# A two-block transformer kernel: GpSimd casts the first weight unit, VectorE makes low parts in one stage, two orders are rewritten

## The chip, the cores and the metric

The program runs on 1 core of one Trainium2 chip. The metric is device time in microseconds (us) of the launch; lower is better. A profiled execution also gives a span, from its first to its last instruction.

## The reference, cut to what matters

Everything is float32, 512 tokens by 1024 features. Two blocks follow each other.

```python
h = rmsnorm(x, norm_mix)
q, k, v, r, lr_f, lr_b, u, g_a, g_b = split(h @ w_in)         # lr_f, lr_b: 16 columns each
log_a_f = log_sigmoid(lr_f @ w_decay_up_fwd + b_decay_fwd) / 16   # and the same backward
...                                                            # gated linear attention, pooling
x = x + merged @ w_out
gate, up = split(rmsnorm(x, norm_ffn) @ w_ffn_in)              # 2 x 2816 columns
x = x + (silu(gate) * up) @ w_ffn_out
x = rmsnorm(x, norm_final)
# second block
mod = silu(c) @ w_ada + b_ada                                  # shift, scale, gate
h = rmsnorm(x, norm_g) * (1 + scale) + shift
...                                                            # dilated attention, HGRN2
x = x + gate * (y @ w_out_2)
out = rmsnorm(x, final_g)
```

## The kernel before, in words

**Products in three parts.** A float32 product is made from matmuls in the fp32r format: each operand is split into a high part (a cast to fp32r) and a low part (the operand minus its high part), and a tile of the result is the sum of high x high, high x low and low x high. The activations' parts are `hhi` and `hlo`, eight slices of 128 features by 512 tokens. The weights come in 112 units of at most 128x2048 elements, 1 MB each. SP loads a unit into `raw[slot]`, two slots in turn. ScalarE casts it to `whi[slot]` (`split_hi`, L456), and GpSimd subtracts and writes `wlo[slot]` (`split_lo`, L460); for some units VectorE does that (`dve_low`, L1225). TensorE waits on the count `s_unit_lo` before it uses a unit and on `s_acc_free` before it writes one of four PSUM banks `acc`; four more banks, `M`, serve all else. Most units hold two tiles of 24 matmuls each (`pe_tile`, L482 to L484), 0.227 us apart.

All order is written by hand: each engine has one list of instructions and waits on semaphores. A wait blocks all that stands behind it on its engine.

**The start.** SP loads x in four tiles, then the narrow weights `wlr` (the 32 columns lr_f and lr_b), the first unit (q and k of head 0) into slot 0, twelve small rows of vectors and the second unit. GpSimd issues ten small loads. x is normalised, transposed on TensorE into eight banks (L1954), scaled by ScalarE into `hhi` (L716), and VectorE writes `hlo` (L1293), slice by slice. Between the transposes TensorE runs matmuls on the identity that no one reads (`keep_clock`, L1925). The order on TensorE is then: 8 `keep_clock` matmuls; the narrow projection (L1970), with the transposition of the vector rows (L1974) amid it; two matmuls for an attention bias (L1995, L1997); the high products of q (`first_hi`, L1982 and L1983: `whi` by `hhi` and by `hlo`); `lr_sum` (L2017), which sums the narrow projection; the high products of k; four matmuls that expand the decay (`decay`, L2011); and the low products of q and k (`first_lo`, L1989). Then `head_iteration(0)` follows: the two tiles of unit 2, with `decay(4)` and `decay(5)` behind the first and `decay(6)`, `decay(7)` behind the second; the values (unit 3, L505 to L507); and unit 4.

ScalarE, behind the slices of `hhi`, casts unit 1, copies rows, evicts the narrow projection (L725), evicts the bias (L727), casts unit 2, copies `lr3` (L731), and runs three functions on each decay matmul (L751 to L755). Behind the fourth of these it evicts q and k (L739) and only then casts unit 3 (`split_hi(act, 3, 0)`). The cast of unit 4 stands ahead of the last decay. VectorE turns each decay into a running sum (L1304 to L1312).

**The first FFN projection.** 22 units of two tiles, gate and up, 11 passes of two. On VectorE a unit's block is: `ada_tile` (four instructions, L1508 to L1515, that reduce a 1024x128 tile of `w_ada`), then fsg (L1525, L1527), faa (L1531) and alo (L1534), the two last for the second tile. TensorE runs one small matmul on each `ada_tile` result, `ada_tile` too (L2190), behind a unit's second tile; it waits for the sum. In the first pass the matmul for unit 0 stands behind the first tile of unit 1.

**The end.** The last projection, `out_part(h, a)`, works on halves h of the columns; for each half, a = 0 and a = 1 are the halves of the contraction, and each runs over four token tiles t, one PSUM bank each (L2444 to L2446). The same four banks serve both h, so tile t of h = 1 waits until VectorE has read the bank in `z_tile(0, t)` (L1801; L1803 adds the residual). `z_square` on ScalarE sums the squares of a tile (L1194). `y_first` on VectorE multiplies it by the gains (L1807); it waits for the squares, since both use the tile.

Of the kernel before, what the change touches and what calls it, by code (L numbers as in the profile page):

```python
# [7 lines left out]
P = 128  # L8
DM = 1024
L = 512  # L10
KT = DM // P
TT = L // P
# [3 lines left out]
LR = 2 * RANK  # L16
# [4 lines left out]
FT = D_FF // P  # L21
# [30 lines left out]
U_LR, U_HEAD, U_C, U_POOL, U_BR, U_OUT = 0, 1, 17, 23, 24, 28  # L52
# [60 lines left out]
def build(nc, inp, out):  # L113
# [18 lines left out]
    ident = at("ident", S0, [P, P])  # L132
# [114 lines left out]
    with ctx:  # L247
# [158 lines left out]
        def later(n):  # L406

            return not isinstance(n, int) or n > 0
# [15 lines left out]
        def x_bank(k):  # L424

            return acc[k] if k < 4 else M[k - 4]
# [46 lines left out]
        def raw_free(sp, u):  # L473
            if later(u - 1):
                sp.wait_ge(s_unit_lo, u - 1)
# [194 lines left out]
        def _(act):  # L670
# [49 lines left out]
            split_hi(act, 1, 0)  # L720
            act.wait_ge(s_col_mm, 2)
            A(vcol[:, KT:P], acc[3][:, KT:P], ACT.Copy).then_inc(s_cols, 1)
            b, full, _ = TL(U_LR, 0)
            act.wait_ge(s_acc_full, full)
            A(lrT[:, :], acc[b][:, :], ACT.Copy).then_inc(s_acc_free[b], 1)  # L725
            act.wait_ge(s_bias_mm, 2)
            A(brow[:, 0:L], M[3][0:A_HEADS, :], ACT.Copy).then_inc(s_bias_row, 1)  # L727
            A(brow[:, L:BW], M[2][0:A_HEADS, 0:BW - L], ACT.Copy).then_inc(s_bias_row, 1)
            split_hi(act, 2, 1)
# [458 lines left out]
            split_hi(act, U_OUT2 + 3, 1, lin=first_tile(U_OUT2) + TT)  # L1188
# [8 lines left out]
            for t in range(TT):  # L1197
                z_square(0, t)
# [14 lines left out]
        def _(dve):  # L1213
# [7 lines left out]
            def dve_low(u, slot):  # L1221

                dve.wait_ge(s_unit_lo, u)
                dve.wait_ge(s_unit_hi, u + 1)
                V.tensor_tensor(wlo[:, slot, :], raw[:, slot, :], whi[:, slot, :].bitcast(f32), ALU.subtract)\  # L1225
                    .then_inc(s_unit_lo, 1)
# [291 lines left out]
            with dve.Fori(0, FT // 2) as i:  # L1518
                for j in range(2):
                    ada_tile(i * 2 + j, j)  # L1520
                    bg, gfull, gfree = TL(U_FIN, 2 * j, 4, i)
                    bu, full, ufree = TL(U_FIN, 2 * j + 1, 4, i)
                    dve.wait_ge(s_norm_rs, 1)
                    dve.wait_ge(s_acc_full, gfull)
                    V.tensor_tensor(fsg[:, j, :], acc[bg][:, :], nrs[:, :], ALU.mult).then_inc(s_f_norm, 1)  # L1525
                    dve.wait_ge(s_f_sig, i * 2 + j + 1)
                    V.tensor_tensor(fsg[:, j, :], fsg[:, j, :], acc[bg][:, :], ALU.mult)\  # L1527
                        .then_inc(s_acc_free[bg], 1)
                    dve.wait_ge(s_acc_full, full)
                    dve.wait_ge(s_acc_free[bg], gfree + 1)  # L1530
                    V.tensor_tensor(faa[:, j, :], fsg[:, j, :], acc[bu][:, :], ALU.mult)\  # L1531
                        .then_inc(s_acc_free[bu], 1)
                    dve.wait_ge(s_f_hi, i * 2 + j + 1)
                    V.tensor_tensor(cols(alo, i * 2 + j), faa[:, j, :], cols(ahi, i * 2 + j).bitcast(f32),  # L1534
                                    ALU.subtract).then_inc(s_f_lo, 1)
            V.tensor_tensor(nrs[:, :], nrs[:, :], nrs[:, :], ALU.mult).then_inc(s_f_norm, 1)
# [277 lines left out]
            for t in range(TT):  # L1814
                z_tile(0, t)
                if t > 0:
                    y_first(t - 1)
            y_first(TT - 1)
# [10 lines left out]
        def _(pool):  # L1829
# [8 lines left out]
            for c in range(3):  # L1838
# [5 lines left out]
                          bass.AP(tensor=e.tensor, offset=0, ap=[[0, P], [1, NG * 2 * PAD]])).then_inc(s_edge_in, 16)  # L1844
            pool.wait_ge(s_wup_in, 6 * 16)
# [6 lines left out]
            split_lo(pool, 1, 0)  # L1852
# [19 lines left out]
            unit_pairs(U_BR, U_FOUT)  # L1872
            unit_pairs(U_FOUT, U_ATT, FT // 2 * P)
# [10 lines left out]
        def _(pe):  # L1884
# [75 lines left out]
            pe.wait_ge(s_lr_in, 32)  # L1960
            b, _, _ = TL(U_LR, 0)
            strips = P // LR
            pe.wait_ge(s_norm_lo, 1)
            keep_clock(acc[b], 8)
            for m in range(KT // strips):
                pe.wait_ge(s_norm_lo, (m + 1) * strips)
                for h in (hhi, hlo):
                    for c in range(strips):
                        k = m * strips + c
                        last = mm(acc[b][c * LR:(c + 1) * LR, :], wlr[:, k, :], h[:, k, :].bitcast(f32),  # L1970
                                  start=(m == 0 and h is hhi), stop=(m == 1 and h is hlo), skip_group_check=True)
                if m == 0:
                    pe.wait_ge(s_rows_in, 12 * 16)
                    nc.tensor.transpose(acc[3][:, 0:P], vrow[:, :], ident[:, :]).then_inc(s_col_mm, 1)  # L1974
                if m == 1:
                    last.then_inc(s_acc_full, 1)

            def first_hi(bank, j):

                for k in range(KT):  # L1980
# [11 lines left out]
            b_q, _, _ = TL(U_HEAD, 0)  # L1992
            b_k, _, _ = TL(U_HEAD, 1)
# [20 lines left out]
            pe.wait_ge(s_unit_hi, U_HEAD + 1)  # L2014
            first_hi(b_q, 0)
            pe.wait_ge(*moved(U_LR, 0))
            mm(M[0][:, :], lr_sum[:, :], lrT[:, :], start=True, stop=True).then_inc(s_lr3, 1)  # L2017
            first_hi(b_k, 1)
# [4 lines left out]
            pe.wait_ge(s_unit_lo, U_HEAD + 1)  # L2023
            first_lo(b_q, 0)
            first_lo(b_k, 1)
# [454 lines left out]
```

## Time and profile before

| what | value |
|---|---|
| median of 3 runs | 1352.64 us (1350.17, 1352.64, 1352.73) |
| the profiled execution, its own time | 1350.47 us |
| its span | 1348.7 us |
| TensorE busy | 1331.6 us, 99% of the span |
| TensorE weight loads | 1096.6 us, 81% |
| VectorE, ScalarE, GpSimd busy | 744.9, 573.8, 442.2 us |
| mean granted TensorE clock | 0.999 |

Times in a profile count from the start of the span. PE is TensorE's matmuls, PEld its weight loads, DVE is VectorE, ACT ScalarE, POOL GpSimd, and SP SyncE with its DMA queue. A number in square brackets behind an instruction is the idle time of its engine before it and what ended it. Matmul ends are modelled: a 512-column matmul shows as 0.39 us, while the next begins 0.227 us later.

### The profile page before, as it was taken

Reading aid. Unit: us, or ns where it says so; the run is one execution under the profiler, and the core shown is the slowest. Engines: PE = TensorE matmul, PEld = TensorE weight load, DVE = VectorE, ACT = ScalarE, POOL = GpSimd, SP = SyncE. Lnnn points to the kernel's source line nnn. Section 1 sums busy time; section 2 is a strip of 40 time slices with the busy share of each in tenths; the row PEclk is TensorE's granted clock in tenths of the full one; section 3 lists DMA queues with packets and bytes.
Section 4 is the critical chain, followed back from the end, with each engine's and each line's share of the span. In section 5 each row is a group of like instructions: output and inputs, shape, how many; then the busy total and the mean of one; then the engine's idle time right before and its main releaser. Section 6 shows DMA issues by size and latency. Waiting matters only on the chain.

```text
span 1348.7 us, 21206 instructions
## 1 busy us (share of the span) xinstructions
PE 1331.6 (99%) x8182; PEld 1096.6 (81%) x8182; DVE 744.9 (55%) x1243; ACT 573.8 (43%) x786; POOL 442.2 (33%) x118
## 2 busy tenths in 40 slices
PE   8999999999999999999999999999999999999997
PEld 6888989888888888888888877777888888888885
DVE  4643242664466888888844472335677777102445
ACT  5644353361243222222323255556555655433233
POOL 5421222234443444444444413322211111444441
PEclk9999999999999999999999999999999999999999
DMA  6231312214235555554433342232232222223221
GB/s 194 88 93 63 93 62 93 93 49 167 86 91 156 140 140 140 140 140 130 117 91 102 105 109 78 83 104 63 64 86 69 62 80 76 65 93 120 99 94 63
DMA packets 201671, 134.31 MB, mean 100 GB/s; under 512 B 5720, under 2 KB 195017, under 8 KB 201623
## 3 DMA queue, kind: packets, MB, share of 16 engines
q1 hardware_dynamic: 200390, 131.41, 33.4%
q10 hardware_dynamic: 848, 1.60, 0.4%
q8 instruction: 33, 0.54, 0.2%
q0 software_dynamic: 384, 0.64, 0.2%
q14 instruction: 16, 0.12, 0.0%
HBM read 131.51 MB, written 2.12 MB: 99 GB/s over the span
## 4 chain that ended last, share of the span: by engine, by line
PE 89%; issue 6%; DVE 2%; POOL 2%; ACT 0%; DMA 0%; POOLq 0%; DVEq 0%; ACTq 0%
PE acc L482 19%; PE acc L483 19%; PE acc L484 19%; PE acc L491 4%; PE acc L493 3%; PE acc L492 3%; POOL wlo L460 2%; PE acc L506 1%; PE acc L505 1%; PE acc L507 1%; PE acc L1905 1%; PE acc L1906 1%; PE acc L1907 1%; PE acc L2444 1%; PE acc L2446 1%
## 5 line engine op out<-in xcount | busy, mean ns | idle before, releaser
L460 POOL TENSOR_TENSOR wlo<-raw,whi 128x2048 fp32r<-128x2048 f32 (+1 forms) x97 | 427.2, 4404 | 864.9 <-ACT whi L456 864.8
L482 PE MATMUL acc<-hhi,whi 128*128 128x512 f32 x928 | 370.4, 399 | 1.9 <-issue 1.9
L484 PE MATMUL acc<-hhi,wlo 128*128 128x512 f32 x928 | 361.6, 390 | 0.0
L483 PE MATMUL acc<-hlo,whi 128*128 128x512 f32 x928 | 361.6, 390 | 0.0
L456 ACT ACTIVATE whi<-raw 128x2048 fp32r<-128x2048 f32 (+1 forms) x110 | 203.6, 1851 | 111.4 <-PE acc L484 92.0
L482 PEld LDWEIGHTS acc<-hhi,whi 128*128 128x128 f32 x928 | 174.3, 188 | 41.2 <-issue 6.5
L483 PEld LDWEIGHTS acc<-hlo,whi 128*128 128x128 f32 x928 | 174.4, 188 | 37.8 <-issue 3.1
L484 PEld LDWEIGHTS acc<-hhi,wlo 128*128 128x128 f32 x928 | 174.2, 188 | 36.7
L1511 DVE TENSOR_TENSOR ada<-ada 128x512 f32<-128x512 f32 x24 | 104.6, 4357 | 0.8
L491 PE MATMUL acc<-hhi,whi 128*128 128x512 f32 x224 | 92.7, 414 | 0.8 <-DVE wlo L1225 0.8
L493 PE MATMUL acc<-hhi,wlo 128*128 128x512 f32 x224 | 87.8, 392 | 0.0
L492 PE MATMUL acc<-hlo,whi 128*128 128x512 f32 x224 | 87.6, 391 | 0.0
L901 ACT ACTIVATE fsg<-fsg 128x512 f32<-128x512 f32 x22 | 13.9, 632 | 136.0 <-DVE fsg L1525 136.0
L482 PE MATMUL acc<-ahi,whi 128*128 128x512 f32 x176 | 68.7, 390 | 0.0
L484 PE MATMUL acc<-ahi,wlo 128*128 128x512 f32 x176 | 68.5, 389 | 0.0
L483 PE MATMUL acc<-alo,whi 128*128 128x512 f32 x176 | 68.5, 389 | 0.0
L491 PEld LDWEIGHTS acc<-hhi,whi 128*128 128x128 f32 x224 | 42.1, 188 | 12.8 <-issue 3.5
L493 PEld LDWEIGHTS acc<-hhi,wlo 128*128 128x128 f32 x224 | 42.0, 188 | 9.7
L492 PEld LDWEIGHTS acc<-hlo,whi 128*128 128x128 f32 x224 | 42.2, 188 | 7.5
L1548 DVE TENSOR_TENSOR ada<-acc,nrs 128x512 f32<-128x512 f32 x16 | 11.0, 690 | 51.6 <-PE acc L484 51.6
L484 PEld LDWEIGHTS acc<-ahi,wlo 128*128 128x128 f32 x176 | 33.0, 188 | 6.9
L482 PEld LDWEIGHTS acc<-ahi,whi 128*128 128x128 f32 x176 | 33.0, 188 | 6.8
(388 smaller groups left out, 2153.3 us busy)
## 6 DMA issues: line engine op xcount, KB each, us to landing
raw<-in_w_in_dram SPq DMA_DIRECT2D x56, 512.0 KB
raw<-in_w_in_dram SPq DMA_DIRECT2D x26, 1024.0 KB
raw<-in_w_ffn_in_dram SPq DMA_DIRECT2D x44, 512.0 KB
ada<-in_w_ada_dram SPq DMA_DIRECT2D x24, 512.0 KB, 3.8
raw<-in_w_ffn_out_dram SPq DMA_DIRECT2D x16, 704.0 KB
raw<-in_w_out_dram SPq DMA_DIRECT2D x8, 1024.0 KB
xnat<-in_x_dram SPq DMA_DIRECT2D x8, 512.0 KB, 6.3
raw<-in_w_branch_gla_dram SPq DMA_DIRECT2D x4, 1024.0 KB
```

The costliest lines, as they stand in the source:

```text
L456: nc.scalar.activation(whi[:, slot, 0:n], raw[:, slot, 0:n], ACT.Copy).then_inc(s_unit_hi, 1)
L460: nc.gpsimd.tensor_tensor(wlo[:, slot, 0:n], raw[:, slot, 0:n], whi[:, slot, 0:n].bitcast(f32), ALU.subtract).then_inc(s_unit_lo, 1)
L482: nc.tensor.matmul(acc[bank][:, :], h, xh[:, k, :], start=(k == 0), stop=False)
L483: nc.tensor.matmul(acc[bank][:, :], h, xl[:, k, :], start=False, stop=False)
L484: last = nc.tensor.matmul(acc[bank][:, :], lo, xh[:, k, :], start=False, stop=(k == nk - 1))
L491: nc.tensor.matmul(acc[bank][:, :], whi[:, slot, ws], hhi[:, k, :], start=(k == 0), stop=False)
L492: nc.tensor.matmul(acc[bank][:, :], whi[:, slot, ws], hlo[:, k, :], start=False, stop=False)
L493: last = nc.tensor.matmul(acc[bank][:, :], wlo[:, slot, ws], hhi[:, k, :], start=False, stop=(k == KT - 1))
L505: nc.tensor.matmul(o, xh[:, k, xs], h, start=(k == 0), stop=False)
L506: nc.tensor.matmul(o, xh[:, k, xs], lo, start=False, stop=False)
L901: A(fsg[:, j, :], fsg[:, j, :], ACT.Sigmoid).then_inc(s_f_sig, 1)
L1511: V.tensor_tensor(w[:, 0:4, :], w[:, 0:4, :], w[:, 4:8, :], ALU.add).then_inc(s_ada_step, 1)
```

## The change

- **Start.** GpSimd casts unit 1 to its high part itself, and makes its low part right behind, ahead of its work on `wup`. ScalarE's cast of unit 1 goes, and its cast of unit 2 comes first in its list, behind a wait for GpSimd's cast. TensorE makes the high products of q and k ahead of the narrow projection, in one loop over the rows k of `hhi` and `hlo`: four matmuls a row. The 8 `keep_clock` matmuls go. Then come the narrow projection, the vector rows, the bias, the low products of q, `lr_sum`, the low products of k, and the four decays. The x transposes use the banks in another order, so that the banks of q and k come free first.
- **Loads.** `raw_free` has no wait any more for unit 2; for all other units the wait is the same.
- **First FFN projection.** The low parts of its units from the third on, and of the first two of the second FFN projection, are made by VectorE, each at the end of a unit's block, so ahead of the next `ada_tile`. GpSimd skips them.
- **End.** VectorE runs all four `z_tile(0, t)` and then all four `y_first(t)`. ScalarE's cast of the last unit moves from ahead of the squares to behind the second.

```diff
@@ -423,7 +423,7 @@
-            return acc[k] if k < 4 else M[k - 4]
+            return acc[(1, 2, 0, 3)[k]] if k < 4 else M[k - 4]
@@ -471,7 +471,7 @@
         def raw_free(sp, u):
-            if later(u - 1):
+            if later(u - 2):
                 sp.wait_ge(s_unit_lo, u - 1)
@@ -717,16 +717,16 @@
-            split_hi(act, 1, 0)
-            act.wait_ge(s_col_mm, 2)
-            A(vcol[:, KT:P], acc[3][:, KT:P], ACT.Copy).then_inc(s_cols, 1)
+            act.wait_ge(s_unit_hi, 2)
+            split_hi(act, 2, 1)
             b, full, _ = TL(U_LR, 0)
...
             A(lrT[:, :], acc[b][:, :], ACT.Copy).then_inc(s_acc_free[b], 1)
+            act.wait_ge(s_col_mm, 2)
+            A(vcol[:, KT:P], acc[3][:, KT:P], ACT.Copy).then_inc(s_cols, 1)
             act.wait_ge(s_bias_mm, 2)
...
             A(brow[:, L:BW], M[2][0:A_HEADS, 0:BW - L], ACT.Copy).then_inc(s_bias_row, 1)
-            split_hi(act, 2, 1)
             act.wait_ge(s_lr3, 1)
@@ -1185,7 +1185,6 @@
             split_hi(act, U_OUT2 + 2, 0, lin=first_tile(U_OUT2))
-            split_hi(act, U_OUT2 + 3, 1, lin=first_tile(U_OUT2) + TT)
@@ -1195,6 +1194,8 @@
             for t in range(TT):
+                if t == 2:
+                    split_hi(act, U_OUT2 + 3, 1, lin=first_tile(U_OUT2) + TT)
                 z_square(0, t)
@@ -1218,11 +1219,11 @@
-            def dve_low(u, slot):
+            def dve_low(u, slot, n=16 * P):
...
                 dve.wait_ge(s_unit_hi, u + 1)
-                V.tensor_tensor(wlo[:, slot, :], raw[:, slot, :], whi[:, slot, :].bitcast(f32), ALU.subtract)\
+                V.tensor_tensor(wlo[:, slot, 0:n], raw[:, slot, 0:n], whi[:, slot, 0:n].bitcast(f32), ALU.subtract)\
                     .then_inc(s_unit_lo, 1)
@@ -1515,7 +1516,7 @@
             dve.wait_ge(s_silu_c, 1)
-            with dve.Fori(0, FT // 2) as i:
+            def gate_up(i, n=16 * P):
                 for j in range(2):
@@ -1533,6 +1534,11 @@
                                     ALU.subtract).then_inc(s_f_lo, 1)
+                    dve_low(i * 2 + (U_FIN + 2 + j), j, n)
+            with dve.Fori(0, FT // 2 - 1) as i:
+                gate_up(i)
+            gate_up(FT // 2 - 1, FT // 2 * P)
             V.tensor_tensor(nrs[:, :], nrs[:, :], nrs[:, :], ALU.mult).then_inc(s_f_norm, 1)
@@ -1813,9 +1819,8 @@
                 z_tile(0, t)
-                if t > 0:
-                    y_first(t - 1)
-            y_first(TT - 1)
+            for t in range(TT):
+                y_first(t)
             V.tensor_scalar(xss, aden[:, 0, :], 1.0 / DM, EPS, ALU.mult, ALU.add).then_inc(s_norm_rs, 1)
@@ -1842,6 +1847,9 @@
                           bass.AP(tensor=e.tensor, offset=0, ap=[[0, P], [1, NG * 2 * PAD]])).then_inc(s_edge_in, 16)
+            pool.wait_ge(s_unit_in[0], 32)
+            nc.gpsimd.tensor_copy(whi[:, 0, :], raw[:, 0, :]).then_inc(s_unit_hi, 1)
+            split_lo(pool, 1, 0)
             pool.wait_ge(s_wup_in, 6 * 16)
@@ -1849,7 +1857,6 @@
             pool.wait_ge(s_pool_prep, 5)
-            split_lo(pool, 1, 0)
             split_lo(pool, 2, 1)
@@ -1869,8 +1876,9 @@
-            unit_pairs(U_BR, U_FOUT)
-            unit_pairs(U_FOUT, U_ATT, FT // 2 * P)
+            unit_pairs(U_BR, U_FIN + 2)
+            pool.wait_ge(s_unit_lo, U_FOUT + 2)
+            unit_pairs(U_FOUT + 2, U_ATT, FT // 2 * P)
             split_lo(pool, U_ATT, 0)
@@ -1957,40 +1965,35 @@
+            b_q, _, _ = TL(U_HEAD, 0)
+            b_k, _, _ = TL(U_HEAD, 1)
+            pe.wait_ge(s_unit_hi, U_HEAD + 1)
+            for k in range(KT):
+                pe.wait_ge(s_norm_lo, max(k, 1) + 1)
+                for bank, j in ((b_q, 0), (b_k, 1)):
+                    h = whi[:, 0, k * 2 * P + j * P:k * 2 * P + (j + 1) * P]
+                    mm(acc[bank][:, :], h, hhi[:, k, :], start=(k == 0), stop=False)
+                    mm(acc[bank][:, :], h, hlo[:, k, :], start=False, stop=False)
+            def first_lo(bank, j):
+                for k in range(KT):
+                    lo = wlo[:, 0, k * 2 * P + j * P:k * 2 * P + (j + 1) * P]
+                    last = mm(acc[bank][:, :], lo, hhi[:, k, :], start=False, stop=(k == KT - 1))
+                last.then_inc(s_acc_full, 1)
...
             strips = P // LR
-            pe.wait_ge(s_norm_lo, 1)
-            keep_clock(acc[b], 8)
             for m in range(KT // strips):
-                pe.wait_ge(s_norm_lo, (m + 1) * strips)
                 for h in (hhi, hlo):
...
                                   start=(m == 0 and h is hhi), stop=(m == 1 and h is hlo), skip_group_check=True)
-                if m == 0:
-                    pe.wait_ge(s_rows_in, 12 * 16)
-                    nc.tensor.transpose(acc[3][:, 0:P], vrow[:, :], ident[:, :]).then_inc(s_col_mm, 1)
-                if m == 1:
-                    last.then_inc(s_acc_full, 1)
-            def first_hi(bank, j):
-                for k in range(KT):
-                    h = whi[:, 0, k * 2 * P + j * P:k * 2 * P + (j + 1) * P]
-                    mm(acc[bank][:, :], h, hhi[:, k, :], start=(k == 0), stop=False)
-                    mm(acc[bank][:, :], h, hlo[:, k, :], start=False, stop=False)
-            def first_lo(bank, j):
-                for k in range(KT):
-                    lo = wlo[:, 0, k * 2 * P + j * P:k * 2 * P + (j + 1) * P]
-                    last = mm(acc[bank][:, :], lo, hhi[:, k, :], start=False, stop=(k == KT - 1))
-                last.then_inc(s_acc_full, 1)
-            b_q, _, _ = TL(U_HEAD, 0)
-            b_k, _, _ = TL(U_HEAD, 1)
+            last.then_inc(s_acc_full, 1)
+            pe.wait_ge(s_rows_in, 12 * 16)
+            nc.tensor.transpose(acc[3][:, 0:P], vrow[:, :], ident[:, :]).then_inc(s_col_mm, 1)
             pe.wait_ge(s_bias_src, 32)
@@ -2011,18 +2014,15 @@
-            pe.wait_ge(s_unit_hi, U_HEAD + 1)
-            first_hi(b_q, 0)
+            pe.wait_ge(s_unit_lo, U_HEAD + 1)
+            first_lo(b_q, 0)
             pe.wait_ge(*moved(U_LR, 0))
             mm(M[0][:, :], lr_sum[:, :], lrT[:, :], start=True, stop=True).then_inc(s_lr3, 1)
-            first_hi(b_k, 1)
+            first_lo(b_k, 1)
             pe.wait_ge(s_pool_prep, 5)
...
                 decay(i)
-            pe.wait_ge(s_unit_lo, U_HEAD + 1)
-            first_lo(b_q, 0)
-            first_lo(b_k, 1)
```

## Rows read from the trace of the kernel before

**Rows 1.** The page, busy time by engine: us, share of the span, instructions
```profile
PE 1331.6 (99%) x8182; PEld 1096.6 (81%) x8182; DVE 744.9 (55%) x1243; ACT 573.8 (43%) x786; POOL 442.2 (33%) x118
```

**Rows 2.** Timeline of the start: start us, us, engine line op
```profile
13.01 0.60 PE L1954 MATMUL mid<-ident,xnat 128*128 128x128 f32 x4
...
14.65 2.02 PE L1925 MATMUL acc<-ident 128*128 128x128 f32 x16 [1.04 <-DVE hlo L1293]
...
15.30 0.54 POOL L1843 DMA_DIRECT2D edge<-in_edge_dram  x1
...
18.61 1.04 POOL L1846 CAST wup<-wup 128x1024 fp32r<-128x1024 f32 x1 [2.77 <-DMA wup<-in_w_decay_up_bwd_dram]
...
22.17 9.16 POOL L460 TENSOR_TENSOR wlo<-raw,whi 128x2048 fp32r<-128x2048 f32 x2
```

**Rows 3.** DMA view of 0 to 13 us: packets, MB, share of 16 engines
```profile
q1 hardware_dynamic: 4040, 3.42, 84.8%
```

**Rows 4.** Chain that ended last, 0 to 60 us: start us, us, what
```profile
19.17 1.92 PE acc L1970 x16
21.09 0.95 PE mid L1995 x2
22.26 0.43 PE acc L1982
...
26.15 0.86 PE mid L2017 x2
...
30.69 0.91 PE mid L2011 x4
31.59 3.63 PE acc L1989 x16
```

**Rows 5.** Timelines of 30 to 100 us (ScalarE, GpSimd) and 46 to 48 us (TensorE)
```profile
31.01 0.69 ACT L751 ACTIVATE lt<-mid,vcol 128x512 f32<-128x512 f32 x1 [3.36 <-PE mid L2011]
...
39.60 1.92 ACT L456 ACTIVATE whi<-raw 128x2048 fp32r<-128x2048 f32 x1
...
41.60 4.62 POOL L460 TENSOR_TENSOR wlo<-raw,whi 128x2048 fp32r<-128x2048 f32 x1 [9.60 <-ACT whi L456]
...
46.84 0.28 PE L505 MATMUL acc<-whi,hhi 128*128 128x256 f32 x1
```

**Rows 6.** Windows at both ends: busy us (count) of each engine, granted clock, DMA
```profile
3.40:3.80 0.40, 0.40 (x3) 0.40 (x3) 0.00 (x0) 0.00 (x0) 0.00 (x0) 1.00 0.97 369
...
7.40:7.80 0.40, 0.40 (x6) 0.40 (x5) 0.40 (x1) 0.37 (x2) 0.00 (x0) 1.00 1.07 440
...
1342.10:1344.80 2.70, 0.00 (x0) 0.00 (x0) 2.01 (x3) 1.94 (x5) 0.00 (x0) 1.00 0.52 194
1344.80:1348.70 3.90, 0.00 (x0) 0.00 (x0) 0.75 (x1) 0.73 (x2) 0.00 (x0) 0.51 0.54 202
```

**Rows 7.** First FFN projection, first pass: timeline; then the line view of L1225
```profile
425.06 1.03 DVE L1534 TENSOR_TENSOR alo<-faa,ahi 128x512 f32 x1 [0.82 <-ACT ahi L904]
...
428.45 0.29 DVE L1515 TENSOR_TENSOR ada<-ada 128x128 f32<-128x128 f32 x1
...
428.80 0.38 PE L2190 MATMUL mid<-one_col,ada 128*128 128x1 f32 x2
...
L1225 DVE TENSOR_TENSOR wlo<-raw,whi x12: 2280/2282/2286, 77.9 to 1135.8; 128x2048 fp32r<-128x2048 f32 x12
```

**Rows 8.** First FFN projection, a later pass: timeline of VectorE and TensorE
```profile
507.64 0.29 DVE L1515 TENSOR_TENSOR ada<-ada 128x128 f32<-128x128 f32 x1
...
508.29 0.28 PE L2190 MATMUL mid<-one_col,ada 128*128 128x1 f32 x2
```

**Rows 9.** Timeline of the end: VectorE, ScalarE and TensorE
```profile
1314.49 0.69 DVE L1803 TENSOR_TENSOR ynat<-ynat,xmn 128x512 f32<-128x512 f32 x1
...
1320.20 4.56 DVE L1807 TENSOR_TENSOR ynat<-ynat,gain_row 128x512 f32<-128x512 f32 x1 [5.02 <-ACT zsq L1194]
...
1317.64 1.92 ACT L456 ACTIVATE whi<-raw 128x2048 fp32r<-128x2048 f32 x1 [9.02 <-PE acc L2446]
...
1325.42 0.50 PE L2444 MATMUL acc<-whi,nhi 128*128 128x512 f32 x1 [2.43 <-DVE ynat L1801]
```

More of the change, by code:

```diff
@@ L1957, in _ @@
                         last.then_inc(s_x_tr, 1)
-            pe.wait_ge(s_lr_in, 32)
-            b, _, _ = TL(U_LR, 0)
-            strips = P // LR
-            pe.wait_ge(s_norm_lo, 1)
-            keep_clock(acc[b], 8)
-            for m in range(KT // strips):
-                pe.wait_ge(s_norm_lo, (m + 1) * strips)
[L1967 to L1971, printed above, removed]
-                if m == 0:
-                    pe.wait_ge(s_rows_in, 12 * 16)
-                    nc.tensor.transpose(acc[3][:, 0:P], vrow[:, :], ident[:, :]).then_inc(s_col_mm, 1)
-                if m == 1:
-                    last.then_inc(s_acc_full, 1)
-            def first_hi(bank, j):
-                for k in range(KT):
+            b_q, _, _ = TL(U_HEAD, 0)
[4 more added lines that the diff above has]
+                for bank, j in ((b_q, 0), (b_k, 1)):
                     h = whi[:, 0, k * 2 * P + j * P:k * 2 * P + (j + 1) * P]
@@ L1990, in first_lo @@
                 last.then_inc(s_acc_full, 1)
-            b_q, _, _ = TL(U_HEAD, 0)
-            b_k, _, _ = TL(U_HEAD, 1)
+            pe.wait_ge(s_lr_in, 32)
+            b, _, _ = TL(U_LR, 0)
+            strips = P // LR
+            for m in range(KT // strips):
+                for h in (hhi, hlo):
+                    for c in range(strips):
+                        k = m * strips + c
+                        last = mm(acc[b][c * LR:(c + 1) * LR, :], wlr[:, k, :], h[:, k, :].bitcast(f32),
+                                  start=(m == 0 and h is hhi), stop=(m == 1 and h is hlo), skip_group_check=True)
+            last.then_inc(s_acc_full, 1)
+            pe.wait_ge(s_rows_in, 12 * 16)
+            nc.tensor.transpose(acc[3][:, 0:P], vrow[:, :], ident[:, :]).then_inc(s_col_mm, 1)
             pe.wait_ge(s_bias_src, 32)
```

## Prediction

> **What bounds the kernel.** I read the page's busy times first: TensorE is busy for 99% of the span [rows 1]. So a step counts only if it makes TensorE start something later or earlier. The next views were the waits of TensorE, which hold one large entry, at the end [rows 9], then the timelines of the three stages that the change touches, and the chain of work for the start, which gives what each piece costs TensorE when nothing holds it up [rows 4]. After each stage I ask where TensorE stands against before; with 99% busy no later stage gives such a shift back, or takes it away.
>
> **Start, TensorE's own order.** The last transpositions of x end at 13.6 us [rows 2]. Before, TensorE went on at 14.65 with matmuls that no one reads, and then with the narrow projection. Now nothing may run until GpSimd has cast unit 1. GpSimd issues its last load until 15.84 [rows 2]. By 13 us SP's queue had moved 3.42 MB, which is x (2.1 MB), the narrow weights and nearly all of unit 1 (1.05 MB) [rows 3], so the cast waits for GpSimd's own queue. A cast of this size by GpSimd is not in the trace; one of half the size took 1.04 us [rows 2]. Bounds: 1.04 us if the size were free, 4.6 us if it cost what its subtraction of this size does (9.16 for two [rows 2]). I take 2.0, as it is the same operation. TensorE starts at 15.84 + 2.0 + 0.1 for the signal = 17.95. VectorE's slices of `hlo` do not hold it: the loop needs one per four matmuls, 0.9 us, and they are complete when the narrow projection could end before, at 19.17 [rows 4].
>
> From there, by the chain [rows 4]: 32 high products at 3.63 / 16 = 0.227 us, and 0.2 for the slow first: 7.5. The narrow projection, whose second half took 1.92: 3.84. The transposition of the vector rows: 0.2. The bias: 22.26 - 21.09 = 1.17. Low products of q 1.82, `lr_sum` 0.86, low products of k 1.82. The first decay starts at 17.95 + 17.2 = 35.2 instead of 30.69, **4.5 us later**, and the four end at 36.1 instead of 35.22. TensorE itself has lost only 0.9: it does the same work, and the fillers and gaps of before were what the order cost. GpSimd's moved work fits in: low part of unit 1 until 22.6, `wup` until 26, unit 2 until 30.7. SP's load of unit 3, which waits for the low part of unit 1, goes out some 4 us sooner, with nothing beside it.
>
> **Start, the chain behind the decay.** ScalarE's first function on a decay stood at 31.01; the fourth, the evictions of q and k, and the cast of unit 3 follow on it without a gap, and that cast began at 39.60. GpSimd's low part ran from 41.60 to 46.22, and TensorE began the values at 46.84 [rows 5]. The slack was 0.6 us. All of this hangs on the first decay, so it moves by 4.5: low part of unit 3 at 50.7, values at 50.8 instead of 46.84. **Cost 3.9 us**, of which 3.1 are a wait of TensorE for GpSimd that is new. Bounds: 0.9 if this chain were not in the way, and 6.5 if the cast took 4.6. The later units' chains move by the same, so nothing else comes late.
>
> **Start, the clock.** TensorE now idles from 13.6 to 17.95, 4.3 us. The trace shows what idling does once: after the last matmul the granted clock is 1.00 until 1344.8 and 0.51 from there, the lower of the two levels, 1.2 GHz for 2.4 [rows 6]. The stretch of 2.7 us ahead of that holds no matmul; the wait of 2.43 us at the end [rows 9] did not do it. So I expect the clock to fall here. How long it stays low: at the kernel's beginning the same filler matmuls run 3 in 0.4 us at 3.4 us and 6 in 0.4 us at 7.4 [rows 6] (the clock column reads 1.00 in both, but the pace is half), so between 1.0 and 4.6 us after the first matmul at 2.8. Half of that is lost: 0.5 to 2.3. I take **1.5 us**, all ahead of the first decay, so all of it counts.
>
> The Trainium skill (TensorE: Matmul & The Clock Gate, section on the HAM clock gate) says that the gate halves the clock once the engine has been idle, and gives it back after sustained work. By that rule the sum contains the loss; by the 2.43 us wait alone it would not. The trace agrees with the rule in the fall at its end.
>
> **Loads.** The wait that `raw_free` drops for unit 2 was for a count that a memset had given long before: nothing, from both sides.
>
> **First FFN projection.** In the steady passes VectorE's sum for `ada_tile` ended at 507.93 and TensorE asked for it at 508.29 [rows 8]. VectorE's low part costs 2.28 us [rows 7] and GpSimd's subtraction, behind which VectorE's instructions with both inputs in SBUF stood still (4.56 us for one that takes 0.69 [rows 9]), goes. So VectorE has more room than before, and TensorE, which waited for neither, gains nothing. The first pass is different. There the low part of the third unit stands ahead of the second `ada_tile`. Before, alo ended at 426.09 and the sum at 428.74, and TensorE used it at 428.80 [rows 7], when it came for it, give or take 0.1. Now: alo without the contention takes 0.69, so until 425.75; low part 2.28; the same 2.65 to the sum: 430.7. **Cost 1.9 us** of new waiting. Bounds: 0 if TensorE arrived 2 us later than I think, and 2.3 if alo is no faster. The next units' sums have more than 1 us to spare. Into the second projection a low part of VectorE ends about 5 us behind the first's last tile, and TensorE needs it after 7.5.
>
> **End.** TensorE waited 2.43 us for `z_tile(0, 2)` [rows 9], because VectorE was in `y_first(0)`, which waited 5.02 us for ScalarE's squares, which stood behind the cast at 1317.64, and then ran 4.56 us against GpSimd. Now VectorE is free from 1315.18 and reads the third and fourth banks as soon as they are full, the last by 1318.5; TensorE needs the third at 1322.8. The wait goes: 2.43, and 0.17 by which a matmul overlaps the next, **gain 2.6**. Next in line is the low part of the last unit, made as before. Bounds: 0 to 2.7. All that follows moves along, the tail behind the last matmul included.
>
> **Sum.** 3.9 + 1.9 - 2.6 = +3.2 us with the clock kept, and +4.7 with its fall. The profiled execution took 1350.47 (span 1348.7 and 1.8 around it): 1355.2 on its scale. The median of the runs, 1352.64, is 2.2 above it; the four executions stand at 1350.2, 1350.5, 1352.6 and 1352.7, and as I don't know which of these levels one of after takes, I add to their mean, 1351.5: **1356.2 us**.
>
> **Rivals.** 0.2%, 2.7 us, is about what a measurement of this kernel can tell from no change.
> - *The clock holds.* For it: the 2.43 us wait left it at 1.00. Against: 2.7 us of idleness ended in 0.51. +3.2: 1354.7. Chance 0.22.
> - *The chain behind the decay is not in the way*, because ScalarE or GpSimd reach unit 3 sooner than I read. Start 0.9, so 0.9 + 1.9 - 2.6 = +0.2: 1351.7. Against: 0.6 us of slack and no gap on ScalarE. Chance 0.08.
> - *The clock stays low for longer*, or falls again in the new 3.1 us wait for unit 3, at 2.3 for each: +7.8: 1359.3. For it: that wait is longer than 2.7. Chance 0.12.
> - *Faster: the steady FFN passes.* VectorE's sum came 0.36 us ahead of TensorE. If in the slower executions of before it comes late in each unit, the change takes that wait away. It decides from (2.7 + 4.7) / 20 = 0.37 us a unit. Against: no such wait in the profiled execution. At 0.4 a unit: -3.3, 1348.2. Chance 0.08.
> - My forecast, with its own range 1354 to 1358.5: 0.50.
>
> **How the numbers follow.** The range 1351.5 to 1360 holds the forecast, the held clock, the longer fall and the unhindered chain; it leaves out the faster case and extremes of the cast's price. Slower by over 0.2%: nearly all of the forecast, all of the longer fall, half of the held clock (+3.2 against 2.7): 0.69. Within: 0.22. Faster: 0.09.
>
> **What the profile after would show.** A gap on TensorE up to about 18 us behind a GpSimd CAST of 128x2048, and matmuls at 0.43 us behind it, if the clock fell. The first decay near 35 to 37. A wait of about 3 us for GpSimd's `wlo` ahead of the first values (L505's successor). A wait of 1.9 us at the second `ada_tile` matmul, none at the later ones. No wait at the end. The prediction fails if the cast is much quicker or slower than 2 us, if the values do not wait, or if the clock holds.

## The result, and the profile after

| | before | after |
|---|---|---|
| median of 14 runs, us | 1351.03 | 1354.24 |
| ratio of the times, 95% interval | | 1.0019 [1.0011, 1.0026] |
| profiled execution: time, span, us | 1350.47, 1348.7 | 1354.96, 1353.2 |
| mean granted clock in it | 0.999 | 0.994 |

The change makes the kernel slower, by 0.19%, which is 2.5 us; the interval lies clear of 1, and the size just under the bound of 0.2% of the forecast. The two medians lie 3.2 us apart; the ratio is not theirs, since before's runs stand in two groups and its median depends on how many fall in each. Two slow runs, one of before at 1658.25 us and one of the start alone (below) at 3440.33, are left out of the ratios. The forecast was 1356.2 with a range that holds 1354.24. The two profiled executions are 4.5 us apart, since that of before is of its lower group and that of after among its slower ones. After ran between 1351.02, at a mean clock of 0.998, and 1355.82, at 0.994, and the time goes with the clock: how often the clock fell makes most of that spread, as I infer, since only one run was profiled.

The page of after, busy time by engine:

```profile
PE 1332.9 (99%) x8166; PEld 1098.5 (81%) x8166; DVE 706.2 (52%) x1265; ACT 571.8 (42%) x785; POOL 345.4 (26%) x97
```

GpSimd's 97 us less and VectorE's 39 us less [rows 1] are no gain by themselves: TensorE is as busy as before. The waits of TensorE in after (total us, times, longest), without those of the kernel's first microseconds:

```profile
PE acc L1975 <- DVE hlo L1294: 4.2, 1, 4.2
...
PE acc L505 <- POOL wlo L460: 2.0, 1, 2.0
PE mid L2190 <- DVE ada L1516: 1.8, 1, 1.8
```

(The profile puts a wait down to the signal that it shows last.) The large wait at the end [rows 9] is gone, and three stand in its place. The first is put down to VectorE's `hlo`, but the timeline of after shows what the matmul waited for, the cast, and what followed:

```profile
15.84 1.90 POOL L1851 CAST whi<-raw 128x2048 fp32r<-128x2048 f32 x1
...
17.80 0.79 PE L1975 MATMUL acc<-hhi,whi 128*128 128x512 f32 x1 [4.18 <-DVE hlo L1294]
...
18.39 0.63 PE L1976 MATMUL acc<-hlo,whi 128*128 128x512 f32 x1
18.82 0.63 PE L1975 MATMUL acc<-hhi,whi 128*128 128x512 f32 x1
...
22.96 0.39 PE L1975 MATMUL acc<-hhi,whi 128*128 128x512 f32 x1
23.19 0.40 PE L1976 MATMUL acc<-hlo,whi 128*128 128x512 f32 x1
...
31.40 1.91 ACT L456 ACTIVATE whi<-raw 128x2048 fp32r<-128x2048 f32 x1 [13.72 <-PE acc L1992]
...
37.28 1.09 PE L2014 MATMUL mid<-lr,wup 128*128 128x512 f32 x4
...
46.36 1.92 ACT L456 ACTIVATE whi<-raw 128x2048 fp32r<-128x2048 f32 x1
...
48.35 4.57 POOL L460 TENSOR_TENSOR wlo<-raw,whi 128x2048 fp32r<-128x2048 f32 x1 [9.63 <-ACT whi L456]
...
52.98 0.39 PE L505 MATMUL acc<-whi,hhi 128*128 128x256 f32 x1 [1.98 <-POOL wlo L460]
```

The matmuls stand 0.43 us apart at 18.4 and 0.23 at 23.0: after 4.2 us of idleness the clock is at its lower level. The chain of the forecast is there step by step: first decay at 37.28 (before 30.69 [rows 4]), the cast of unit 3 at 46.36, its low part, and the values 0.06 us behind its end, at 52.98 instead of 46.84 [rows 5]. One thing I had not read in the diff: ScalarE's cast of unit 2 also waits for the count of finished tiles (`s_acc_full`), so until the narrow projection is done, and starts at 31.40. My forecast had its low part ready at 30.7. It came in time, by 0.15 us: its low part ended at 38.05 and TensorE took the unit up at 38.2.

Windows of after (busy us and count of PE, PEld, DVE, ACT, POOL; granted clock; DMA share; GB/s):

```profile
16.20:22.60 6.40, 4.80 (x11) 3.80 (x12) 2.90 (x5) 1.48 (x3) 6.32 (x3) 0.50 0.63 207
51.00:53.00 2.00, 0.02 (x1) 0.02 (x1) 1.97 (x3) 1.94 (x4) 1.93 (x1) 1.00 0.05 12
53.60:56.80 3.20, 3.20 (x17) 3.20 (x17) 3.04 (x4) 3.17 (x4) 0.94 (x1) 0.50 0.79 225
57.00:60.00 3.00, 3.00 (x27) 3.00 (x27) 2.86 (x4) 0.65 (x2) 3.00 (x1) 1.00 0.41 96
439.40:442.50 3.10, 3.10 (x9) 2.45 (x8) 1.96 (x3) 1.55 (x3) 0.00 (x0) 0.50 0.77 222
443.00:446.00 3.00, 3.00 (x15) 2.48 (x14) 2.40 (x2) 0.57 (x1) 0.00 (x0) 1.00 0.83 238
```

TensorE is busy throughout the third and the fifth row, but gets through 17 and 9 matmuls where the rows behind them have 27 and 15. Each stands half a microsecond to a microsecond behind a wait of 2.0 or 1.8 us. So the clock fell three times, not once; the second and the third fall lasted about 3.5 us, at a cost of some 1.6 us each. The unit in which the third fell took 12.90 us, and 11.31 in the kernels below in which the clock holds there.

The timeline of after in the first FFN projection: the first pass, then a turn of the loop.

```profile
432.78 0.69 DVE L1535 TENSOR_TENSOR alo<-faa,ahi 128x512 f32 x1 [0.83 <-ACT ahi L904]
433.39 2.28 DVE L1226 TENSOR_TENSOR wlo<-raw,whi 128x2048 fp32r<-128x2048 f32 x1
...
438.03 0.29 DVE L1516 TENSOR_TENSOR ada<-ada 128x128 f32<-128x128 f32 x1
...
438.38 0.38 PE L2190 MATMUL mid<-one_col,ada 128*128 128x1 f32 x2 [1.83 <-DVE ada L1516]
...
484.66 0.28 PE L2190 MATMUL mid<-one_col,ada 128*128 128x1 f32 x2
484.80 0.48 PE L482 MATMUL acc<-hhi,whi 128*128 128x512 f32 x1
...
495.79 0.28 PE L2190 MATMUL mid<-one_col,ada 128*128 128x1 f32 x2
```

The same turn before:

```profile
519.42 0.31 PE L2190 MATMUL mid<-one_col,ada 128*128 128x1 f32 x2
...
519.93 0.49 PE L482 MATMUL acc<-hhi,whi 128*128 128x512 f32 x1 [0.21 <-issue]
...
530.94 0.28 PE L2190 MATMUL mid<-one_col,ada 128*128 128x1 f32 x2
```

In the first pass the low part costs a wait of 1.83 us. In the passes behind it lies what I missed. After, a unit takes TensorE 11.13 us each time (484.66 to 495.79), and the matmul behind the `ada_tile` starts 0.14 later. Before, units took 11.13 and 11.52 in turn (508.29 [rows 8], 519.42, 530.94), with 0.51 us at the turn, a mean of 11.33. Over the 19 units that is 0.2 x 19 = 3.8 us. Among TensorE's waits of before it shows only in part, and with no releaser:

```profile
PE acc L482 <- issue: 1.9, 9, 0.3
```

The accounts of the two profiled executions, in us:

| term | predicted | profile of after |
|---|---|---|
| start, with the clock kept | +3.9 | +3.9 |
| fall of the clock at the start | +1.5 | +2.2 |
| second fall, behind the wait for unit 3 | 0 | +1.6 |
| first FFN pass | +1.9 | +1.8 |
| third fall, behind that wait | 0 | +1.6 |
| steady FFN passes | 0 | -3.8 |
| end | -2.6 | -2.7 |
| sum | +4.7 | +4.6 (measured 4.5) |

The 3.9 is the values at 50.78 in a run that kept the clock (below), against 46.84; the 2.2 are what 52.98 stands above that.

### The profile page after: what moved, and what is told of

The parts are those of the page before. It is cut to its first block, busy times and chain, and to the rows that moved or that the text cites. A ratio compares the mean times of both kernels' runs of the same rounds, so it can differ in the third digit from the quotient of the medians.

```text
span 1353.2 us, 21147 instructions
## 1 busy us (share of the span) xinstructions
PE 1332.9 (99%) x8166; PEld 1098.5 (81%) x8166; DVE 706.2 (52%) x1265; ACT 571.8 (42%) x785; POOL 345.4 (26%) x97
## 4 chain that ended last, share of the span: by engine, by line
PE 87%; issue 7%; DVE 3%; POOL 2%; ACT 1%; DMA 0%; SPq 0%; POOLq 0%; DVEq 0%; ACTq 0%
PE acc L482 18%; PE acc L483 18%; PE acc L484 18%; PE acc L491 4%; PE acc L493 3%; PE acc L492 3%; POOL wlo L460 2%; PE acc L505 1%; PE acc L506 1%; PE acc L507 1%; PE acc L1913 1%; PE acc L1915 1%; PE acc L2446 1%; PE acc L2445 1%; PE acc L1914 1%
## 5 line engine op out<-in xcount | busy, mean ns | idle before, releaser
L460 POOL TENSOR_TENSOR wlo<-raw,whi 128x2048 fp32r<-128x2048 f32 (+1 forms) x75 | 328.5, 4380 | 972.2 <-ACT whi L456 972.1
L1226 DVE TENSOR_TENSOR wlo<-raw,whi 128x2048 fp32r<-128x2048 f32 (+1 forms) x34 | 76.5, 2251 | 20.6 <-ACT whi L456 20.6
L505 PE MATMUL acc<-whi,hhi 128*128 128x256 f32 x128 | 37.8, 295 | 2.0 <-POOL wlo L460 2.0
```

Source lines behind the costliest of these rows:

```text
L460: nc.gpsimd.tensor_tensor(wlo[:, slot, 0:n], raw[:, slot, 0:n], whi[:, slot, 0:n].bitcast(f32), ALU.subtract).then_inc(s_unit_lo, 1)
L505: nc.tensor.matmul(o, xh[:, k, xs], h, start=(k == 0), stop=False)
L1226: V.tensor_tensor(wlo[:, slot, 0:n], raw[:, slot, 0:n], whi[:, slot, 0:n].bitcast(f32), ALU.subtract)\
```

## The experiments

### Each part by itself

Three kernels take one part of the change each, on the kernel before: the hunks of the start and the loads, those of the first FFN projection, those of the end.

> The kernel before with only the start of the change (and the load wait that goes with it). My theory now: TensorE reaches the values of head 0 at 53.0 us instead of 46.84 (+6.2: 0.9 by its own order, 2.4 by the lower clock from 16 to 22.8 us, the rest a wait for the low part of unit 3), and the wait of 2.0 us there lets the clock fall once more, +1.5. So +6 to +8 us against before, in most runs. The rival, that the start costs its own order alone (+0.9) and what was lost came from the FFN stage, gives +1.

> The kernel before with only the FFN part: VectorE makes the low parts. My theory: a wait of 1.9 us in the first pass, 1.5 for the clock that it lets fall, and 10 loop turns that are 0.4 us shorter each: -0.6 us, same within 0.2%, and without the fall of the clock -2. The matmul behind the sum of the small tile is to find its sum 2.6 us ahead, and the period is to be 11.13 us in all units (before 11.13 and 11.53 in turn). A rival, that the shorter turns came from something in the start of the whole change, shows the turns unchanged, and +2 to +3.

> The kernel before with only the end reordered. My theory: the wait of 2.43 us is gone: -2.6 us against the profiled execution of before; where the wait of before let the clock fall in a run, -4. The rival: the wait moves (to the last low part of GpSimd, or to ScalarE's later cast): 0.

| part | median, us | ratio to before, 95% interval | ratio in us |
|---|---|---|---|
| start | 1358.5 | 1.0051 [1.0038, 1.0064] | +6.9 |
| first FFN | 1351.84 | 1.0002 [0.9993, 1.0011] | +0.3 |
| end | 1348.05 | 0.998 [0.9972, 0.9989] | -2.7 |

The sum of the parts is +4.5, the whole +2.5. The intervals are wide enough to hold that difference, but the traces also show a place for it. The first two keep the 2.43 us wait at the end. Windows of the start alone, behind that wait:

```profile
1330.00:1334.00 4.00, 1.57 (x7) 1.00 (x6) 3.97 (x3) 0.00 (x0) 2.31 (x1) 1.00 0.00 0
1334.50:1337.80 3.30, 3.30 (x9) 2.53 (x9) 2.96 (x6) 1.17 (x4) 0.00 (x0) 0.50 0.00 0
```

and of the FFN alone:

```profile
1326.20:1329.40 3.20, 3.20 (x9) 2.45 (x9) 2.98 (x5) 1.40 (x4) 0.00 (x0) 0.50 0.03 5
```

In both the clock falls there. From the end of that wait to the end of the span, the start alone takes 24.9 us and the FFN alone 24.8, and before, whose clock held, 23.3 (1348.7 - 1325.42): the fall costs 1.6 us. Of the kernel before 24 runs on one chip stand in two groups, 1349.6 to 1350.4 and 1351.6 to 1352.5, and the profiled one, of the lower group, kept its clock there [rows 9]. The end alone has no such wait and one group, 1347.6 to 1348.4. So the wait at the end, as I infer, sometimes costs before a fall of the clock too: all runs of the lower group have mean clocks of 0.998 or 0.999, those of the upper group 0.997. No run of the upper group was profiled, and the groups lie about 2 us apart, 0.4 more than the fall costs where a trace shows it.

The start alone shows the wait for unit 3 and the falls behind the cast and behind that wait, as after does. The FFN alone shows the 1.8 us wait, a fall of the clock behind it, and 11.13 us a unit from there: +1.8, +1.6, -3.8 come to -0.4, against +0.3 measured, and that includes the fall at the end.

### Is it the late sum that costs the steady passes?

Before, VectorE's sum came 0.36 us ahead of TensorE's use [rows 8]. One theory: it is simply late, and the cure is to let TensorE ask later. The rival: VectorE, ScalarE and GpSimd form a ring that needs 11.3 us a unit whoever waits for it. This kernel is the one before with the `ada_tile` one tile of TensorE later:

```diff
             def gate_up(i, j):
                 tile(U_FIN, 2 * j, j, 0, 4, i)
+                ada_tile(i * 2 + j - 1, 1 - j)
                 tile(U_FIN, 2 * j + 1, j, 1, 4, i)
-                ada_tile(i * 2 + j, j)
```

> The kernel before, but TensorE's small matmul on each reduced tile of w_ada stands behind the first tile of the next unit in every pass, not behind the unit it belongs to. No low part moves. My theory, that the turns of TensorE's loop cost 0.4 us because the sum that it waits for comes 0.2 us ahead, so that its sequencer can't run ahead of the matmuls: the sum is now 5 us old, the ten turns lose their 0.4 us each, -4 us. The rival, that the turns got shorter because GpSimd no longer reads and writes SBUF beside TensorE or because VectorE's loop is another, gives 0 here.

It took 1354.38, ratio 1.0032 [1.0021, 1.0044], slower by 4.3 us instead of faster by 4. Timeline of this kernel, TensorE early in the loop and later in it:

```profile
478.38 0.28 PE L2190 MATMUL mid<-one_col,ada 128*128 128x1 f32 x2
...
489.50 0.28 PE L2190 MATMUL mid<-one_col,ada 128*128 128x1 f32 x2
489.64 0.48 PE L482 MATMUL acc<-hhi,whi 128*128 128x512 f32 x1
...
579.86 0.28 PE L2190 MATMUL mid<-one_col,ada 128*128 128x1 f32 x2
...
585.32 0.39 PE L484 MATMUL acc<-hhi,wlo 128*128 128x512 f32 x1
585.66 0.49 PE L482 MATMUL acc<-hhi,whi 128*128 128x512 f32 x1
...
591.24 0.28 PE L2190 MATMUL mid<-one_col,ada 128*128 128x1 f32 x2
```

and its VectorE, ScalarE and GpSimd in one of the later units:

```profile
576.87 0.69 DVE L1527 TENSOR_TENSOR fsg<-fsg,acc 128x512 f32<-128x512 f32 x1 [0.70 <-ACT fsg L901]
...
578.94 1.90 ACT L456 ACTIVATE whi<-raw 128x2048 fp32r<-128x2048 f32 x1
580.91 4.61 POOL L460 TENSOR_TENSOR wlo<-raw,whi 128x2048 fp32r<-128x2048 f32 x1 [6.68 <-ACT whi L456]
581.05 5.02 DVE L1511 TENSOR_TENSOR ada<-ada 128x512 f32<-128x512 f32 x1
...
588.16 0.69 DVE L1527 TENSOR_TENSOR fsg<-fsg,acc 128x512 f32<-128x512 f32 x1 [0.70 <-ACT fsg L901]
```

For six units TensorE runs at 11.13 with 0.14 us at the turn, as the first theory says. GpSimd subtracts beside it there as before, so that it uses SBUF at the same time as TensorE is not what slows TensorE. But the sum's lead shrinks, from 5.4 to 4.3 us, and then TensorE is back at 11.3 (579.86 to 591.24 is 11.38). It is now held at the start of each unit by GpSimd's low part, which ends at 585.52, 0.14 us ahead of the unit's first matmul at 585.66; from 506 to 642 us every unit starts 0.05 or 0.14 us behind such an end, where before the low part had a lead of 1.8 to 2.1 us. The gap is small: 0.34 us from one matmul to the next at 585.32, where 0.23 is the rule. VectorE's own period is 11.3 here too (576.87 to 588.16). The ring reads off the second fence, in which VectorE waits for nothing but ScalarE's short functions: `fsg` and `faa`, ScalarE's `ahi` and behind it its cast, GpSimd's subtraction behind the cast, VectorE's L1511 beside that for 5.0 us, and only then the next `fsg`. Once around takes 11.3 us, longer than TensorE's 11.13, and the ring delivers both the small tile's sum and the low part. Moving TensorE's use of the sum by a tile only lent it time, until the low part came last. After takes the 5.0 us out of the ring: GpSimd has no work beside L1511. The line view of after in the same stretch, 445 to 660 us (us, mean ns, idle before):

```profile
L1512 DVE TENSOR_TENSOR ada<-ada 128x512 f32<-128x512 f32 x20 | 13.8, 692 | 0.7
...
L1532 DVE TENSOR_TENSOR faa<-fsg,acc 128x512 f32<-128x512 f32 x19 | 13.1, 688 | 17.4 <-PE acc L484 17.4
```

and of before:

```profile
L1511 DVE TENSOR_TENSOR ada<-ada 128x512 f32<-128x512 f32 x19 | 93.9, 4941 | 0.7
...
L1531 DVE TENSOR_TENSOR faa<-fsg,acc 128x512 f32<-128x512 f32 x19 | 13.1, 687 | 1.4
```

The same instruction, one step of `ada_tile`, takes 0.69 us instead of 4.94. Before, VectorE hardly waits ahead of `faa`; after, it waits 17.4 us for TensorE. TensorE leads after and followed before. The Trainium skill (SBUF — State Buffer, section "Who interferes with whom") says that a VectorE instruction with two inputs in SBUF contends with a GpSimd instruction that reads SBUF for a shared pair of ports, that the pair is held exclusively, and that the order of issue decides who is blocked. The trace agrees: the subtraction started first, at 580.91, and kept its 4.6 us, and L1511 beside it took 5.02, until 0.55 us behind the subtraction's end.

The run also pays for something else. At the turn to the second projection SP's load of an `ada` tile waits for the later matmul, and with it the weights behind it in that queue. The waits of SP's queue in 640 to 690 us:

```profile
SPq L602 <- PE mid L2190: 18.3, 2, 12.8
```

ScalarE's cast of the next unit then waits for its load until 668.29, where before's cast stood at 663.28, TensorE waits 3.6 us for GpSimd's `wlo`, and the clock falls at 672.3 us. With 1.6 us for the fall that is more than the 3.75 us by which this profiled execution is slower than before's, so it accounts for the kernel being slower and not just no faster.

### The clock at the start

Matmuls that no one reads, ahead of the wait for the cast, keep TensorE busy:

```diff
+            pe.wait_ge(s_norm_lo, 1)
+            keep_clock(acc[b_q], 26)
             pe.wait_ge(s_unit_hi, U_HEAD + 1)
```

> The whole change, with 26 filler matmuls on the identity (as the kernel has them elsewhere, results unread) in TensorE's idle stretch from 14.5 to 17.8 us. My theory: the low clock from 16 to 22.8 us costs 2.4 us ahead of the first decay; with it kept, the first decay stands at 35.2 instead of 37.3. The wait for the low part of unit 3 stays, 2 to 3 us, and may still let the clock fall, 1.5. So -2 to -2.5 against the whole change, about 1352. The rival, that the start is bound by GpSimd's and ScalarE's chain and not by TensorE's pace, leaves the first values at 53.0 us and the time as it is.

1354.46, ratio 1.0027 [1.0016, 1.0037]: no better than after. The timeline of this kernel says why:

```profile
15.19 6.07 PE L1933 MATMUL acc<-ident 128*128 128x128 f32 x52 [0.94 <-DVE hlo L1294]
...
21.02 0.47 PE L1977 MATMUL acc<-hhi,whi 128*128 128x512 f32 x1
```

The 26 calls are 52 records of 0.117 us. They filled 6.07 us and held the high products back by 3.2 us (21.02 against 17.80): nearly what the two falls of the clock had cost there, 2.2 and 1.6. With 12 of them:

> The whole change with 12 fillers. 26 took 6.07 us, since each is two passes of 0.117 us, and held the high products back to 21.0; 12 take 2.8 us and end at about 17.9, as the cast does. Theory: the high products start at 18.0 at full pace, the first decay 2.4 us sooner than in the whole change (near 35), the values at about 50.8 instead of 53.0. So 1352, 2.2 below the whole change, if the wait for unit 3 does not let the clock fall, and 1353.5 if it does. The rival, that keeping the clock by fillers brings nothing since GpSimd's and ScalarE's chain sets the values, gives 1354.2.

Timeline of the kernel with 12:

```profile
15.23 2.94 PE L1933 MATMUL acc<-ident 128*128 128x128 f32 x24 [0.94 <-DVE hlo L1294]
...
17.93 0.47 PE L1977 MATMUL acc<-hhi,whi 128*128 128x512 f32 x1
...
35.08 1.09 PE L2016 MATMUL mid<-lr,wup 128*128 128x512 f32 x4
...
50.78 0.39 PE L505 MATMUL acc<-whi,hhi 128*128 128x256 f32 x1 [1.99 <-POOL wlo L460]
```

1352.15, ratio 1.0009 [1.0, 1.0018], against 1.0019 for after, so the falls of the clock at the start are worth about 0.1%. With the clock kept the first decay is at 35.08 and the values at 50.78; the prediction had 35.2 and 50.8. So its working of the start was right and only the clock's price was low, 1.5 for 2.2 (37.28 - 35.08). And though the wait for unit 3 is still 2.0 us, no fall follows it in the profiled execution, which is one of the faster four (1351.2 to 1351.6, at 0.998); the other seven, up to 1353.5 and at 0.996 or 0.997, may have one.

### The chain behind the decay

ScalarE casts unit 3 ahead of the third decay, and unit 2 without the wait for the narrow projection:

```diff
-            split_hi(act, 2, 1)
+            split_hi(act, 2, 1, lin=0)
...
             for i in range(8):
                 if i == 4:
                     head_evict_qk(0)
+                if i == 2:
                     split_hi(act, 3, 0)
```

> The same with fillers, and ScalarE casts unit 3 ahead of the third decay instead of behind the fourth's functions and the evictions; its cast of unit 2 no longer waits for the narrow projection. My theory: the wait of TensorE for the low part of unit 3 goes, and with it the second fall of the clock: the values start near 48.3 us (before 46.84, the whole change 53.0), so another -2 to -4, about 1349. The rival, that the values would then wait for something else of the same time (the decays' running sums), gives no more than the fillers alone.

1352.78, ratio 1.0007 [0.9998, 1.0016], with 26 fillers. The wait for unit 3 is gone: the values start at 50.73 where the kernel with 26 fillers alone had 53.88. That is 2.4 us later than the 48.3 that I expected, since 26 fillers are too many, and the time missed the expected 1349. Of the 3.15 us at the values only 1.7 are left in the medians: a wait of 1.2 us for ScalarE's `sig_ga` eviction appears at 63.6 us, so what was pushed back on ScalarE is late next. TensorE's wait of 0.5 us for VectorE's `b_all`, amid the later decays, stands there as it does in after.

### Repairing the FFN's first pass

GpSimd makes the low part of the third unit as before, and VectorE starts with the fourth:

```diff
-                    dve_low(i * 2 + (U_FIN + 2 + j), j, n)
+                    if j or not isinstance(i, int) or i:
+                        dve_low(i * 2 + (U_FIN + 2 + j), j, n)
...
-            with dve.Fori(0, FT // 2 - 1) as i:
+            gate_up(0)
+            with dve.Fori(1, FT // 2 - 1) as i:
...
             unit_pairs(U_BR, U_FIN + 2)
+            split_lo(pool, U_FIN + 2, 0)
```

First with 26 fillers, the earlier casts and the rest of after, then with 12:

> The kernel just before, and GpSimd makes the low part of the third unit of the first FFN projection, so that VectorE's reduction of the second small tile is not behind it. My theory: the wait of 1.9 us in the first pass goes, and the fall of the clock behind it (1.5): -3.4, about 1345.5, with the period still 11.13 us in all later units. The rival, that the period goes back to 11.33 because GpSimd's work beside VectorE's sets it off, gives +4.

> The whole change with 12 fillers, the casts of units 2 and 3 earlier, and GpSimd making the third FFN unit's low part. Theory: the kernel with 26 fillers, 1349.7, less the 3 us by which they were too many: 1346.7. That is 2.5 above the kernel with the old start (1344.2), of which 0.9 is TensorE's own order; the rest is to show as the two waits that the kernel with 26 fillers has in head 0 (0.5 for the running sums, 1.2 for an eviction by ScalarE). The rival, that the new start equals the old once it is mended, gives 1344.2.

They took 1349.68, ratio 0.9988 [0.9979, 0.9997], and 1346.8, ratio 0.997 [0.9957, 0.9982]. The first missed its 1345.5, which was set before the kernel that it builds on had run (1352.78 where 1349 was expected); against that kernel it is 3.1 us faster, for 3.4 expected. The units behind the first pass take 11.13 us in both, so the rival is out. Next, the old start with this FFN and the new end:

> The kernel before with its own start, the end reordered, and the FFN part with GpSimd making the third unit's low part. My theory: 0 at the start, -4 in the FFN stage (20 units at 11.13 instead of 11.33), -2.6 at the end: 1343.7, and no fall of the clock. It is to be 1 to 2 us ahead of the kernel with the new start, which costs TensorE 0.9 and the narrow gaps of the decays. The rival, that the new start is worth something once its clock and its wait are mended, has it behind.

It took 1344.19, ratio 0.9948 [0.9934, 0.9961], 7 us faster than before, with runs between 1343.47 and 1344.48 and a clock of 0.999. Its timeline has the values and the second `ada_tile` where before had them [rows 5, 7]:

```profile
46.58 0.28 PE L505 MATMUL acc<-whi,hhi 128*128 128x256 f32 x1
...
428.53 0.38 PE L2199 MATMUL mid<-one_col,ada 128*128 128x1 f32 x2
```

The repaired new start costs 1346.8 - 1344.19 = 2.6 us against the old one, in two sets of runs whose medians of before differ by 0.3. Its waits for `sig_ga` and `b_all`, 1.2 and 0.5 us, are still there, and the values start at 48.74, 2.2 us later than with the old start. So no version of the new start that I tried pays.

## Why the prediction was right where it was, and wrong where it was not

The total came near by luck: two misses of about 4 us each cancel. Of its three outcomes the forecast gave 0.69 to slower by over 0.2%; what came, 0.19%, had 0.22.

**Right: the start's two chains.** GpSimd's own queue as what holds the cast (15.84 to 17.74), the cast at 1.9 us for 2.0, TensorE at 17.80 for 17.95, the step of 17.2 us to the first decay, and the slack of 0.6 us ahead of the values. The kernel with 12 fillers shows the same times without the clock's share. TensorE's wait for unit 3 was 2.0 us and not 3.1: "TensorE itself has lost only 0.9" was too low. With the clock kept it asks for the values at 48.8, 2.0 us later than before, of which 0.5 are the wait for `b_all`, which I had not counted. The values, which carry the cost, were where I had put them.

**Too small: the clock.** "I take 1.5 us, all ahead of the first decay": it was 2.2 there, and 5.4 with the other two falls. The rival "falls again in the new wait for unit 3" came true in the profiled execution, although I had set that wait at 3.1 and priced the fall at 2.3 (it is 1.6). I had taken 2.43 us of waiting as too short for a fall, from one execution that kept its clock. The runs of before already stood on two levels 2.2 us apart. I named them, but did not ask what could differ between two executions of one program; the rows on hand had two candidates, the clock and the steady passes, and I weighed only the second.

**Right: the first FFN pass**, 1.83 us for 1.9. I did not ask whether the clock falls behind it: 1.6 more, in each of the five traces that have this wait.

**Wrong: "So VectorE has more room than before, and TensorE, which waited for neither, gains nothing."** TensorE did wait: 0.2 us a unit, as "issue" and not as a wait with a releaser. What I took for an extra was the brake: VectorE stood still beside GpSimd's subtraction for 4.3 us a unit (4.94 for 0.69), and that made the ring 11.33 us long. A sum that ends 0.36 us ahead of its use, in every pass of a loop, means that the side which makes it is as slow as the side which uses it. I read it as slack. The rival for this had the place right but its evidence wrong: "no such wait in the profiled execution". It also priced it at 0.4 us a unit, twice what it is. Worth 3.8 us, it is just what kept the misses on the clock from showing in the total: without it after would stand near 1358 (1354.24 + 3.8). The test of the periods of two successive units, 11.13 and 11.52, was open before the change.

**Right: the end**, 2.7 for 2.6. By the runs it is worth more than the wait, since the falls of the clock behind the wait go too.

So the forecast came near by two misses that nearly cancel: +3.9 from the clock (2.2 + 1.6 + 1.6 - 1.5) and -3.8 from the steady passes. On the scale of the profiled executions the forecast was 1355.2 and after's took 1354.96. The 2 us between 1356.2 and 1354.24 I put down, without a test, to adding a sum made on profiled executions to the mean of before's levels: in after the wait that makes two levels of before is gone, and nine of the fourteen runs of after had, by their mean clocks of 0.995 to 0.998, a shorter or rarer low clock than the profiled one at 0.994.

**Open:** why a wait of 2.0 or 2.4 us is followed by a fall of the clock in some executions and not in others, and the 0.4 us by which before's groups lie further apart than a fall costs.

## What to carry to other kernels

Where a result comes a few tenths of a microsecond ahead of its use in each pass of a loop, measure the period of single passes before calling it slack: a ring of other engines may be setting it, and the profile may show that as "issue". Make a change in parts: here one of three paid clearly, one paid once its first pass was left out, and the third cost what the others had brought. In a kernel like this, count each new wait of about 2 us on TensorE as one that may cost another 1.6 us for the clock, and look for it at the levels between which the runs of a kernel jump.

## What the runs showed of the hardware

Short waits can cost the clock. In the profiled executions, falls to 1.2 GHz, half of 2.4, of some 3.5 us each followed the wait of 1.8 us in all five kernels that have it (after, the FFN alone, and three kernels with fillers), the wait of 2.0 us in after and the start alone, and the wait of 2.43 us in the start alone and the FFN alone. No fall followed the wait of 2.0 us in the kernels with 26 and 12 fillers, nor that of 2.43 us in before and in the kernel with the later `ada_tile`. By the Trainium skill (TensorE: Matmul & The Clock Gate, section on the HAM clock gate) the gate halves the clock once the engine has idled and restores it after sustained work; the trace agrees in the direction of each fall. GpSimd's cast of 128x2048 took 1.90 us, as ScalarE's does (1.91), and its subtraction of the same size 4.6, for which VectorE takes 2.28: of the two halves of a unit the cast is the one that suits GpSimd.
